# Order of the matmuls with stationary weights: four of 512 columns, then four of 256, instead of pairs

## The chip, the cores and the metric

The kernel runs on one core of a Trainium2 chip. A core has five engines that take their own instruction lists and meet through semaphores: PE (TensorE, the matrix engine, with its weight loads shown apart as PEld), DVE (VectorE), ACT (ScalarE), POOL (GpSimd) and SP (SyncE, which issues most transfers here). The metric is the device time of one execution in microseconds.

## The reference

Two transformer blocks, one after the other, on 256 tokens of 2048 features, all in float32. Cut to the products:

```python
# first block: stick-breaking attention, then a squared-ReLU MLP
qkv = rms_norm(x) @ w_qkv                     # 2048 -> 6144
x = x + attention(qkv) @ w_o                  # 2048 -> 2048
x = x + square(relu(rms_norm(x) @ w1)) @ w2   # 2048 -> 8192 -> 2048
# second block: chunked attention and pooling, then a gated MLP with a causal convolution
z = rms_norm(x) @ w_in                        # 2048 -> 4096
x = x + rms_norm(concat(attention(z), pool(z)) @ w_o)
up = conv3(rms_norm(x) @ w_up)                # 2048 -> 11264
x = x + rms_norm((gelu(up[:5632]) * up[5632:]) @ w_down)
```

The two attention cores, the pooling and the norms are small beside these products.

## The kernel before

Float32 products are made from rounded parts. Every activation tile has a high part and a low part side by side, 256 tokens each, so 512 columns; every weight has a high part `Wh` and a low part `Wl`. A product is high times high, low times high and high times low.

The weights come in 745 **pieces**. A piece is 256 rows of a weight matrix by a strip of 512 output features (128 partitions by 1024 numbers, 512 KB). SP loads a piece into `raw` (6 buffers), ACT rounds it into `Wh` (line 811), DVE takes the rest into `Wl` (line 1023), and PE multiplies by both; there are 5 buffers of `Wh` and `Wl`. A plan written at build time fixes what every engine does in which order: up to four pieces are split ahead of the one that PE works on, and the evacuations, norms and attention steps are laid between the pieces. PE waits on the low part of a piece once, ahead of its first matmul, and the piece's last matmul releases its buffers (`p.mm`) and, in the last piece of a strip, the accumulated result.

There are three kinds of piece:

- **T pieces**, 576 of them, `feature_products`: the weights are stationary, the activations move. The piece has two slices of 128 weight rows (`t`), and each slice has four blocks of 128 output features (`m`), one to each of the four PSUM banks of the accumulator `P`. For each `m` there is a matmul with `Wh` over all 512 columns (high and low activations), and one with `Wl` over the 256 columns of the high activations, into the first half of the same bank. The four pairs of one slice are a row of four, so there are 1152 such rows.
- **N pieces**, `row_products`: the activations are stationary, the weights move. They consist of matmuls of 512 columns only.
- Two **P pieces**, `group_products`, for the pooling, with 8 pairs each.

In the trace a T pair is `ps<-aHL,Wh` (512 columns) and `ps<-aHL,Wl` (256 columns), or the same with `hid` or `oHL` as the moving tensor. All carry line 1332, which is the helper `mm`. Each matmul has its own weight load of 128 columns (LDWEIGHTS on PEld).

Of the kernel before, what the change touches and what calls it, by code (L numbers as in the profile page):

```python
# [11 lines left out]
TOK = 256  # L12
# [634 lines left out]
def build(nc, A, out):  # L647
    with ExitStack() as ctx:
# [84 lines left out]
        def attention_weights(g, blk, h, b, n):  # L733
            if blk == 1:
                return A1[:, g % 2, :, :].rearrange("p h n -> p (h n)").rearrange("p (b h q) -> p b h q", b=3, h=4)[:, b:b + n, h, :]
            return A2[:, g % 2, h, b * 128:(b + n) * 128]
# [593 lines left out]
        def tensor_program(e):  # L1330
            def mm(o, l, r, start, stop):
                return e.matmul(o, l, r, start=start, stop=stop, skip_group_check=True)  # L1332

            def tp(o, i):
                return e.transpose(o, i, ident[:, :])  # L1335

            def row_products(q, row, P):

                wh, wl, mov, kt = Wh[:, q["n"] % NW, :], Wl[:, q["n"] % NW, :], movs[q["mov"]], q["kt"]
                for t in range(2):  # L1340
                    c = slice(t * 512, (t + 1) * 512)
                    hi = mov[:, kt + t, row * 128:(row + 1) * 128]
                    lo = mov[:, kt + t, TOK + row * 128:TOK + (row + 1) * 128]
                    mm(P[:, row, :], hi, wh[:, c], q["first"] and t == 0, False)
                    mm(P[:, row, :], hi, wl[:, c], False, False)
                    m = mm(P[:, row, :], lo, wh[:, c], False, q["last"] and t == 1)
                return m

            def feature_products(q, P, half=None):

                wh, wl, mov, kt = Wh[:, q["n"] % NW, :], Wl[:, q["n"] % NW, :], movs[q["mov"]], q["kt"]
                for t in range(2):
                    if half:
                        e.wait_ge(*half[t])
                    x = mov[:, kt + t, :]
                    for m in range(4):
                        c = slice(t * 512 + m * 128, t * 512 + (m + 1) * 128)
                        mm(P[:, m, :], wh[:, c], x, q["first"] and t == 0, False)
                        r = mm(P[:, m, 0:TOK], wl[:, c], x[:, 0:TOK], False, q["last"] and t == 1)
                return r  # L1360

            def group_products(q, P):
# [10 lines left out]
            for st in p.steps:  # L1373
                k = st["kind"]
                if k == "products":
                    q = pieces[st["i"]]
                    P = ps[q["set"]]
# [4 lines left out]
                    if q["kind"] == "T":  # L1382
                        feature_products(q, P, (st["half"], st["lo"]) if st["half"] else None).then_inc(p.mm, 1)
                    elif q["kind"] == "P":
                        group_products(q, P).then_inc(p.mm, 1)
                    else:
                        for row in st["rows"]:
                            m = row_products(q, row, P)
                            if row == 0 and st["row0"]:
                                m.then_inc(p.row0, 1)  # L1390
                            if row == 1:
                                m.then_inc(p.mm, 1)
                elif k == "rms":
                    P = ps[st["set"]]
# [4 lines left out]
                    for t in range(2):  # L1399
                        m = mm(P[:, 0, t:t + 1], Z4[:, 0, t * 128:(t + 1) * 128], ones[:, 0:1], True, True)  # L1400
                    m.then_inc(st["total"][0], 1)
                elif k == "rms_pair":
                    P = ps[st["set"]]
# [5 lines left out]
                    for j in range(2):  # L1409
                        for t in range(2):  # L1410
                            m = mm(P[:, 0, 2 * j + t:2 * j + t + 1], Z4[:, j, t * 128:(t + 1) * 128], ones[:, 0:1], True, True)
# [12 lines left out]
                elif k == "sb_scores":  # L1424
                    g, P = st["g"], ps[st["set"]]
                    q, kk = qk[:, g % 2, 0, :, :], qk[:, g % 2, 1, :, :]
                    for t in st["need"]:
                        e.wait_ge(*t)
                    for h in range(4):
                        for b, (i, j) in enumerate(BLOCKS):  # L1430
                            m = mm(P[:, b, h * 128:(h + 1) * 128], kk[:, h, i * 128:(i + 1) * 128],
                                   q[:, h, j * 128:(j + 1) * 128], True, True)
                    m.then_inc(st["mm"][0], 1)
                elif k == "sb_weights":
                    g, P = st["g"], ps[st["set"]]
                    for t in st["need"]:
                        e.wait_ge(*t)
                    for b, terms in enumerate((((tri_r, 0),), ((tri_r, 1), (ones_r, 2)), ((tri_r, 2),))):
                        for n, (l, at) in enumerate(terms):
                            c = slice(at * 512, (at + 1) * 512)  # L1440
                            mm(P[:, b, :], l[:, :], E_hi[:, g % 2, c], n == 0, False)
                            m = mm(P[:, b, :], l[:, :], E_lo[:, c], False, n == len(terms) - 1)
                    m.then_inc(st["mm"][0], 1)
                elif k == "values":
                    g, blk, P = st["g"], st["blk"], ps[st["set"]]
# [3 lines left out]
                    for h in range(4):  # L1449
                        c = slice(h * 128, (h + 1) * 128)  # L1450
                        mm(P[:, h, 0:256], v[:, g % 2, 0, c], attention_weights(g, blk, h, 0, 2), True, False)
                        m = mm(P[:, h, 128:256], v[:, g % 2, 1, c], attention_weights(g, blk, h, 2, 1), False, True)
                    m.then_inc(st["mm"][0], 1)
                elif k == "sm_scores":
                    g, P = st["g"], ps[st["set"]]
                    q, kk = qk[:, g % 2, 0, :, :], qk[:, g % 2, 1, :, :]
                    for t in st["need"]:
                        e.wait_ge(*t)
                    for h in range(4):
                        mm(P[:, h, 0:128], q[:, h, 0:128], kk[:, h, 0:128], True, True)  # L1460
                        m = mm(P[:, h, 128:384], q[:, h, 128:256], kk[:, h, :], True, True)
                    m.then_inc(st["mm"][0], 1)
                elif k == "sm_turn":
                    for t in st["need"]:
                        e.wait_ge(*t)
                    for h in range(4):
                        for b in range(3):
                            m = tp(ps[st["set"]][:, h, b * 128:(b + 1) * 128], Z3[:, h, b * 128:(b + 1) * 128])
                    m.then_inc(st["mm"][0], 1)
                elif k == "mixed_norm":  # L1470
                    for n in range(14):
                        m = mm(ps[st["set"]][:, 3, 0:128], ones[:, :], ones[:, :], True, True)
                    m.then_inc(st["warm"][0], 1)
                elif k == "mixed_tiles":
                    j0, b0, P = st["j0"], st["b0"], ps[st["set"]]
                    for t in st["need"]:
                        e.wait_ge(*t)
                    for n, i in enumerate((0, 2)):
                        for a in range(2):
                            for t in range(2):  # L1480
                                j = j0 + i + a
                                m = mm(P[:, b0 + n, a * 256 + t * 128:a * 256 + (t + 1) * 128], xn[:, t, j * 128:(j + 1) * 128],
                                       D[:, t * 128:(t + 1) * 128], True, True)
                        m.then_inc(st["turns"][n][0], 1)
                elif k == "turn_x3":
                    c = st["c"]
# [3 lines left out]
                    for t in range(2):  # L1490
                        for j in range(8):
                            m = tp(ps[st["set"]][:, 2 * t + j // 4, (j % 4) * 128:(j % 4 + 1) * 128],
                                   xT[:, 8 * c + j, t * 128:(t + 1) * 128])
# [56 lines left out]
```

## Time and profile before

| | |
|---|---|
| median of 3 runs | 2157.34 us |
| lowest and highest | 2157.23 and 2159.55 us |
| the profiled execution, its own time | 2159.01 us |
| its span, first to last instruction | 2157.3 us |
| outside the span | 1.7 us |
| mean granted TensorE clock | 0.997 |
| PE busy | 2132.7 us, 99%, 11698 matmuls |
| PE weight loads busy | 1850.3 us, 86% |
| DVE busy | 1285.3 us, 60% |
| ACT busy | 1065.0 us, 49% |

A matmul's record begins where it is started and reaches past the start of the next one, since matmuls are pipelined. So a duration of 0.39 us is not what a matmul costs; what it costs is the distance from its start to that of the next. Where the records of one form follow each other, a count over a stretch, or the first and last start, gives that distance.

### The profile page before, as it was taken

The numbers are of one execution on the slowest core, as the hardware profiler recorded it, in microseconds if no ns is written. First come the engines' busy times: TensorE is split into PE (matmuls) and PEld (weight loads), VectorE is DVE, ScalarE is ACT, GpSimd is POOL, SyncE is SP. The second block draws the span as 40 slices with busy tenths as digits, with TensorE's granted clock in tenths as the row PEclk, the third lists the DMA queues.
The fourth block names the chain that finished last, engine by engine and source line by source line (L and its number), as shares of the span: only waits on it lengthen the run. The fifth ranks groups of instructions, "written<-read, shape, count | busy, mean of one in ns | idle before, by whom it ended". The sixth has DMA issues, their size and how long they took to land.

```text
span 2157.3 us, 28152 instructions
## 1 busy us (share of the span) xinstructions
PE 2132.7 (99%) x11698; PEld 1850.3 (86%) x11698; DVE 1285.3 (60%) x1335; ACT 1065.0 (49%) x1198; POOL 240.5 (11%) x135
## 2 busy tenths in 40 slices
PE   8999999999999999999999999999999999999998
PEld 7888888888888888888888888888888888888886
DVE  6555556655555565555669655576666644566654
ACT  6554554545334443444554545455455433554553
POOL 2000000100000000000224000032222100222211
PEclk9999999999999999999999999999999999999999
DMA  8456555565666655665565655645655666566563
GB/s 274 152 167 190 170 174 185 167 207 174 207 190 183 197 185 190 176 207 193 187 198 172 183 169 177 193 137 186 189 191 180 213 194 193 168 186 200 193 199 111
DMA packets 207472, 399.50 MB, mean 185 GB/s; under 512 B 12400, under 2 KB 15600, under 8 KB 207088
## 3 DMA queue, kind: packets, MB, share of 16 engines
q1 hardware_dynamic: 207056, 395.60, 57.9%
q8 instruction: 92, 1.51, 0.3%
q10 hardware_dynamic: 288, 2.10, 0.2%
q14 instruction: 36, 0.29, 0.0%
HBM read 395.55 MB, written 2.10 MB: 184 GB/s over the span
## 4 chain that ended last, share of the span: by engine, by line
PE 95%; POOL 1%; issue 1%; DVE 1%; ACT 1%; DMA 0%; SPq 0%; DVEq 0%; POOLq 0%; ACTq 0%
PE ps L1332 94%; POOL T L1301 0%; PE ps L1335 0%; DMA raw<-in_sb_w_qkv_dram 0%; DVE raw L1230 0%; DVE Wl L1023 0%; POOL E L1257 0%; POOL T L1303 0%; POOL QK L1264 0%; POOL E L1292 0%; ACT Wh L811 0%; POOL zs L1267 0%; POOL QK L1257 0%; DVE T L978 0%; DVE xT L1101 0%
## 5 line engine op out<-in xcount | busy, mean ns | idle before, releaser
L1023 DVE TENSOR_TENSOR Wl<-raw,Wh 128x1024 fp32r<-128x1024 f32 x745 | 919.9, 1254 | 623.2 <-ACT Wh L811 622.4
L1332 PE MATMUL ps<-aHL,Wh 128*128 128x512 f32 x3328 | 1167.5, 395 | 11.5 <-DVE Wl L1019 6.6
L811 ACT ACTIVATE Wh<-raw 128x1024 fp32r<-128x1024 f32 x745 | 769.1, 1054 | 613.7 <-PE ps L1332 609.3
L1332 PE MATMUL ps<-aHL,Wl 128*128 128x256 f32 x3328 | 932.7, 280 | 0.0
L1332 PEld LDWEIGHTS ps<-aHL,Wh 128*128 128x128 f32 x3328 | 625.8, 188 | 155.6 <-DVE aHL L1013 6.5
L1332 PEld LDWEIGHTS ps<-aHL,Wl 128*128 128x128 f32 x3328 | 630.2, 189 | 0.4
L1332 PE MATMUL ps<-hid,Wh 128*128 128x512 f32 x1024 | 355.1, 391 | 0.0
L1332 PE MATMUL ps<-hid,Wl 128*128 128x256 f32 x1024 | 286.7, 280 | 0.0
L1332 PEld LDWEIGHTS ps<-hid,Wh 128*128 128x128 f32 x1024 | 191.5, 187 | 42.0
L1332 PE MATMUL ps<-Wh,hid 128*128 128x512 f32 x704 | 217.6, 389 | 0.0
L1332 PEld LDWEIGHTS ps<-hid,Wl 128*128 128x128 f32 x1024 | 193.5, 189 | 0.0
L1332 PEld LDWEIGHTS ps<-Wh,hid 128*128 128x128 f32 x704 | 132.1, 188 | 27.3
L1332 PE MATMUL ps<-Wl,hid 128*128 128x512 f32 x352 | 137.0, 389 | 0.0
L1332 PE MATMUL ps<-Wh,aHL 128*128 128x512 f32 x384 | 121.4, 392 | 0.5 <-DVE Wl L1023 0.5
L1257 POOL TENSOR_TENSOR E<-E 128x512 f32<-128x512 f32 x8 | 11.6, 1452 | 954.3 <-ACT E L815 954.3
L1310 POOL TENSOR_TENSOR T<-T,r_b 128x1024 f32<-128x1024 f32 x22 | 71.0, 3229 | 400.2 <-DVE T L978 392.4
L978 DVE TENSOR_TENSOR T<-ps,T 128x1024 f32<-128x1024 f32 x54 | 66.0, 1223 | 55.8 <-ACT T L785 54.3
L1332 PE MATMUL ps<-oHL,Wh 128*128 128x512 f32 x272 | 94.6, 394 | 0.0
L785 ACT ACTIVATE T<-ps 128x1024 f32<-128x1024 f32 x54 | 55.2, 1022 | 67.2 <-PE ps L1332 66.6
L1332 PEld LDWEIGHTS ps<-Wh,aHL 128*128 128x128 f32 x384 | 72.1, 188 | 15.9 <-DVE Wl L1023 0.9
L1332 PE MATMUL ps<-Wh,oHL 128*128 128x512 f32 x256 | 79.5, 390 | 0.0
L1332 PEld LDWEIGHTS ps<-Wl,hid 128*128 128x128 f32 x352 | 66.1, 188 | 13.7
(170 smaller groups left out, 1287.3 us busy)
## 6 DMA issues: line engine op xcount, KB each, us to landing
raw<-in_mlp_w_dram SPq DMA_DIRECT2D x256, 512.0 KB, 4.2
raw<-in_w_up_dram SPq DMA_DIRECT2D x176, 512.0 KB, 3.9
raw<-in_sb_w_qkv_dram SPq DMA_DIRECT2D x95, 512.0 KB, 4.6
raw<-in_w_down_dram SPq DMA_DIRECT2D x88, 512.0 KB, 4.1
raw<-in_w_in_dram SPq DMA_DIRECT2D x64, 512.0 KB, 4.1
raw<-in_sb_w_o_dram SPq DMA_DIRECT2D x32, 512.0 KB, 4.4
raw<-in_w_o_dram SPq DMA_DIRECT2D x32, 512.0 KB, 4.0
xT<-in_x_dram SPq DMA_DIRECT2D x8, 256.0 KB, 7.5
```

The costliest lines, as they stand in the source:

```text
L785: e.activation(T0[:, :, :], ps[st["set"]][:, :, TOK:2 * TOK], ACT.Copy).then_inc(st["copied"][0], 1)
L811: e.activation(Wh[:, i % NW, :], rawv[:, i % NRAW, :], ACT.Copy).then_inc(st["hi"][0], 1)
L978: e.tensor_tensor(T1[:, :, :], ps[st["set"]][:, :, 0:TOK], T0[:, :, :], ALU.add).then_inc(st["summed"][0], 1)
L1023: e.tensor_tensor(Wl[:, i % NW, :], rawv[:, i % NRAW, :], Wh[:, i % NW, :].bitcast(F32), ALU.subtract).then_inc(st["lo"][0], 1)
L1257: e.tensor_tensor(B[:, 0:2, :], B[:, 0:2, :], B[:, 2:4, :], ALU.add).then_inc(st["half"][0], 1)
L1310: e.tensor_tensor(T1[:, :, :], T1[:, :, :], rows4("r_b"), ALU.mult).then_inc(st["done"][0], 1)
L1332: return e.matmul(o, l, r, start=start, stop=stop, skip_group_check=True)
```

## The change

In `feature_products` the loop over the four blocks `m` is cut in two. Before, each turn issued the 512-column matmul with `Wh` and then the 256-column matmul with `Wl` of the same block. Now the four matmuls with `Wh` come first, one to each bank, and then the four with `Wl`.

```diff
                     x = mov[:, kt + t, :]
+                    cs = [slice(t * 512 + m * 128, t * 512 + (m + 1) * 128) for m in range(4)]
                     for m in range(4):
-                        c = slice(t * 512 + m * 128, t * 512 + (m + 1) * 128)
-                        mm(P[:, m, :], wh[:, c], x, q["first"] and t == 0, False)
-                        r = mm(P[:, m, 0:TOK], wl[:, c], x[:, 0:TOK], False, q["last"] and t == 1)
+                        mm(P[:, m, :], wh[:, cs[m]], x, q["first"] and t == 0, False)
+                    for m in range(4):
+                        r = mm(P[:, m, 0:TOK], wl[:, cs[m]], x[:, 0:TOK], False, q["last"] and t == 1)
                 return r
```

On PE, at the start of the program, where the first piece has a wait ahead of each slice, the list before reads:

```order
1 L1332 MATMUL ps<-aHL,Wh 128x512 [waits s_half_lo,s_tile_lo]
2 L1332 MATMUL ps<-aHL,Wl 128x256
3 L1332 MATMUL ps<-aHL,Wh 128x512
4 L1332 MATMUL ps<-aHL,Wl 128x256
5 L1332 MATMUL ps<-aHL,Wh 128x512
6 L1332 MATMUL ps<-aHL,Wl 128x256
7 L1332 MATMUL ps<-aHL,Wh 128x512
8 L1332 MATMUL ps<-aHL,Wl 128x256
9 L1332 MATMUL ps<-aHL,Wh 128x512 [waits s_w_lo]
10 L1332 MATMUL ps<-aHL,Wl 128x256
```

and after the change, at the same place:

```order
1 L1332 MATMUL ps<-aHL,Wh 128x512 [waits s_half_lo,s_tile_lo]
2 L1332 MATMUL ps<-aHL,Wh 128x512 x3
3 L1332 MATMUL ps<-aHL,Wl 128x256 x4
4 L1332 MATMUL ps<-aHL,Wh 128x512 [waits s_w_lo]
5 L1332 MATMUL ps<-aHL,Wh 128x512 x3
6 L1332 MATMUL ps<-aHL,Wl 128x256 x4
7 L1332 MATMUL ps<-aHL,Wh 128x512 [waits s_w_lo,s_tile_lo]
```

The waits stand before the same matmul as before, the first of a slice; only the seven behind it have changed places.

On PE, where the strips of the gated MLP's first half end and the N pieces of the down projection (`ps<-Wh,hid`) begin, before:

```order
8735 L1332 MATMUL ps<-aHL,Wh 128x512
8736 L1332 MATMUL ps<-aHL,Wl 128x256
8737 L1332 MATMUL ps<-aHL,Wh 128x512
8738 L1332 MATMUL ps<-aHL,Wl 128x256
8739 L1332 MATMUL ps<-Wh,hid 128x512
8740 L1332 MATMUL ps<-Wl,hid 128x512
```

and after:

```order
2784 L1332 MATMUL ps<-aHL,Wl 128x256 x4
2785 L1332 MATMUL ps<-aHL,Wh 128x512 x4
2786 L1332 MATMUL ps<-aHL,Wl 128x256 x4
2787 L1332 MATMUL ps<-Wh,hid 128x512
2788 L1332 MATMUL ps<-Wl,hid 128x512
```

The last matmul of the strip is the same one as before, with `Wl` of block 3, and the N pieces behind it have not moved. The numbers of matmuls of each form are the same in both kernels, and ACT, DVE, POOL and SP have the same lists.

## Rows read from the trace of the kernel before

**Rows 1.** The page: PE and weight loads, and the chain by engine.

```profile
PE 2132.7 (99%) x11698; PEld 1850.3 (86%) x11698; DVE 1285.3 (60%) x1335; ACT 1065.0 (49%) x1198; POOL 240.5 (11%) x135
PE 95%; POOL 1%; issue 1%; DVE 1%; ACT 1%; DMA 0%; SPq 0%; DVEq 0%; POOLq 0%; ACTq 0%
```

**Rows 2.** Groups, PE: line, form, count | busy us, mean ns | idle before.

```profile
L1332 PE MATMUL ps<-aHL,Wh 128*128 128x512 f32 x3328 | 1167.5, 395 | 11.5 <-DVE Wl L1019 6.6 <-DVE T L978 3.2 <-DVE aHL L1185 1.3
L1332 PE MATMUL ps<-aHL,Wl 128*128 128x256 f32 x3328 | 932.7, 280 | 0.0
```

**Rows 3.** Timeline, PE, T pieces, from 600 us: start us, us, what.

```profile
599.91 0.39 PE L1332 MATMUL ps<-hid,Wh 128*128 128x512 f32 x1
600.14 0.28 PE L1332 MATMUL ps<-hid,Wl 128*128 128x256 f32 x1
600.25 0.39 PE L1332 MATMUL ps<-hid,Wh 128*128 128x512 f32 x1
...
602.68 0.39 PE L1332 MATMUL ps<-hid,Wh 128*128 128x512 f32 x1
```

**Rows 4.** Timeline, PEld, weight loads of the same stretch.

```profile
600.14 0.19 PEld L1332 LDWEIGHTS ps<-hid,Wh 128*128 128x128 f32 x1
600.26 0.19 PEld L1332 LDWEIGHTS ps<-hid,Wl 128*128 128x128 f32 x1
```

**Rows 5.** Timeline, PE, N pieces, matmuls of 512 columns alone.

```profile
2100.37 0.39 PE L1332 MATMUL ps<-Wl,hid 128*128 128x512 f32 x1
2100.59 0.61 PE L1332 MATMUL ps<-Wh,hid 128*128 128x512 f32 x2
2101.05 0.39 PE L1332 MATMUL ps<-Wl,hid 128*128 128x512 f32 x1
...
2102.41 0.39 PE L1332 MATMUL ps<-Wl,hid 128*128 128x512 f32 x1
```

**Rows 6.** Timeline, PE, T pieces at the lower clock.

```profile
1184.34 0.63 PE L1332 MATMUL ps<-aHL,Wh 128*128 128x512 f32 x1
1184.77 0.41 PE L1332 MATMUL ps<-aHL,Wl 128*128 128x256 f32 x1
1184.98 0.63 PE L1332 MATMUL ps<-aHL,Wh 128*128 128x512 f32 x1
```

**Rows 7.** Timeline, PE, first five and last four of 24 matmuls of the scores.

```profile
63.67 0.72 PE L1332 MATMUL ps<-QK 128*128 128x128 f32 x5
...
65.89 0.61 PE L1332 MATMUL ps<-QK 128*128 128x128 f32 x4
```

**Rows 8.** Stretches: us, then PE, PEld, DVE, ACT, POOL busy (count), PEclk, DMA, GB/s.

```profile
14.00:44.00 30.00, 30.00 (x172) 26.00 (x171) 21.70 (x23) 22.08 (x27) 9.11 (x7) 1.00 0.88 306
450.00:600.00 150.00, 150.00 (x867) 132.25 (x866) 85.53 (x72) 68.93 (x67) 0.00 (x0) 1.00 0.60 196
1500.00:1650.00 150.00, 150.00 (x867) 132.29 (x866) 95.05 (x120) 78.78 (x94) 38.45 (x11) 1.00 0.60 190
1850.00:2000.00 150.00, 150.00 (x851) 130.13 (x850) 91.62 (x113) 78.55 (x94) 36.47 (x10) 1.00 0.59 186
1808.00:2034.00 226.00, 226.00 (x1281) 196.06 (x1280) 138.38 (x168) 114.81 (x134) 47.51 (x13) 1.00 0.59 183
```

**Rows 9.** Stretch at the lower clock, the columns of rows 8.

```profile
1184.50:1186.50 2.00, 2.00 (x8) 1.71 (x7) 2.00 (x3) 0.00 (x0) 0.00 (x0) 0.50 0.49 171
```

**Rows 10.** Timeline, PE, T pieces in the stretch with fewer matmuls.

```profile
1899.70 0.40 PE L1332 MATMUL ps<-aHL,Wh 128*128 128x512 f32 x1
...
1900.76 0.40 PE L1332 MATMUL ps<-aHL,Wh 128*128 128x512 f32 x1
...
1901.82 0.40 PE L1332 MATMUL ps<-aHL,Wh 128*128 128x512 f32 x1
```

## Prediction, made before the run

> **What bounds the kernel now.** I read the page first. PE is busy 99% of the span and holds 95% of the chain that ended last [rows 1]. The groups then say where PE ever stood idle: 11.5 us before the first form of T matmul, nothing before the second [rows 2]. So no semaphore, transfer or other engine is worth asking about. The time is the sum of the distances between matmul starts, and the change can only act through those. The durations in the groups (395 and 280 ns) overlap and are of no use for this; the timeline's starts are.
>
> In T pieces at 600 us the starts of the 512-column matmuls go from 599.91 to 602.68 over 8 pairs: 346 ns a pair, split 0.23 + 0.11 or 0.12 [rows 3]. The count over 150 us says the same: 867 matmuls are 173 ns each, 346 ns a pair [rows 8]. Over 150 us the rounding is small, and a few overlapping records at the edges make the count about two too high; with 865 it is 346.8. I use 346.7. In N pieces, 512 columns only, 9 matmuls take 2102.41 - 2100.37 = 2.04 us, 226.7 ns each [rows 5]. If a 512-column matmul costs the same in a T pair, the 256-column one costs 346.7 - 226.7 = 120 ns.
>
> What part of this is streaming? At a granted clock of 0.50 (the 1.2 GHz level) a pair takes 1184.98 - 1184.34 = 0.64 us [rows 6, 9], so 0.32 us at the 2.4 GHz level if nothing is added. Measured there is 346.7: 26.7 ns above it, for two matmuls. For the N matmul the same ratio gives 320 x 512/768 = 213.3, and 226.7 is 13.4 above it. So every matmul, long or short, carries about 13.3 ns besides its columns, at the full clock alone. A fixed charge for each matmul with its weight load fits all three rows.
>
> Each load starts with the matmul ahead of it (600.14 and 600.26, against matmuls at 600.14 and 600.25) and is 190 ns long on record, yet the 512-column matmul starts 0.11 us after the load for it [rows 3, 4]. So the record's length is not what a load holds up. The pace of loads shows in the attention scores, where 24 matmuls of 128 columns follow each other, each with its load: from the first at 63.67 to the 21st at 65.89 are 20 distances, 111 ns each [rows 7]. I take 112 as the most that a load can hold up. It lies below 120.
>
> **The change part by part.** *Matmuls and loads*: none is added or removed. A row of four is 4 x 226.7 + 4 x 120 = 1386.8 ns before. After, it has the same eight in another order. With a charge per matmul the sum is the same to the nanosecond: difference 0, times 1152 rows, 0 us.
>
> *Cover of the loads.* A load runs beside the matmul ahead of it. Before, four loads lay under 512-column matmuls and four under 256-column ones. After, it is still four and four, since the cover is given by the matmul ahead, and the same eight are ahead of something. The four under short ones have 120 ns of cover for 112 ns of need. What is new is that three of them follow each other. A load starts only once the matmul ahead starts, so a surplus under a long matmul was never carried over and none is lost: 0 us. In the scores, 24 loads went in a row at their pace [rows 7], so issuing instructions keeps up with four short matmuls too.
>
> *PSUM.* Before, both matmuls of a pair went to the same bank; after, each goes to another bank than the one ahead. N pieces write one bank six times in a row at 226.7 ns, with the same 13.3 ns charge as T pairs that change bank every second time [rows 3, 5]. So a bank has no price here either way: 0 us.
>
> *Waits and releases.* The waits stand ahead of the first matmul of a slice as before, and the last matmul of a piece is the same instruction, so the buffers of `Wh` and `Wl` and the strip's result come free when they did. DVE is busy 60%, ACT 49% [rows 1]; nothing in their work moves. 0 us.
>
> *The rhythm.* One thing in the trace isn't explained by a fixed charge. From 1808 to 2034 us the T pieces run slower with the same instructions: 851 matmuls in 150 us where 867 ran before [rows 8]. Three pairs take 1900.76 - 1899.70 = 1.06 us, 353.3 ns a pair [rows 10]. It isn't the company of other engines: 1500 to 1650 us holds the same stage's work (POOL 38.45 against 36.47 us, ACT 78.78 against 78.55) and runs at 867 [rows 8]. So a stream of pairs can settle into either of two rhythms, 6.7 ns a pair apart. What a new order settles into isn't in this trace. Bounds: if all slow stretches went, the one of rows 8 gives 226/353.3 x 6.7 = 4.3 us and the one from 14 to 44 us (172 matmuls, where the usual pace has 173 and the two at the edges, 175) 0.6 us. A few others are shorter; I put them at 50 us together, 0.9 us, so 5.8 us in all. If all T pairs took the slow rhythm, 4608 pairs less some 870 already slow (306 us / 353.3) make 3740 x 6.7 = 25.1 us more. I take 0 between them: the steady form is by far the more common.
>
> *Sum*: 0 us on the span of 2157.3 us of the profiled execution, whose own time was 2159.01. The median of the runs is 2157.34, and the forecast is made on that: 2157.3 us. The runs of before differ by 2.3 us, so a change under 0.2% (4.3 us) can't be told from none.
>
> **The rivals.**
>
> *Short matmuls in a row run at the load pace (faster).* The 120 ns is a difference between two forms; no row shows a 256-column matmul behind another. If a run of them needs only its load pace, 3 of the 4 fall from 120 to 112: 24 ns a row, x 1152 = 27.6 us, 2129.7 us. If they only fall to the 0.117 seen between starts [rows 3], it is 3 x 3.3 x 1152 = 11.4 us, 2145.9 us. For it: the distances 0.23 and 0.117 leave it open how the charge is shared. Against: 226.7 in N pieces fixes the long one at 13.3 ns, and the rest must then be in the short one.
>
> The Trainium skill, TensorE: Matmul & The Clock Gate, Back-to-back issue gap, lists 262 cycles for 256 columns, which is 109 ns at 2.4 GHz, and its section LDWEIGHTS (loading the stationary operand) has a load of 128 columns take 128/1.2 = 107 ns. An estimate from that page puts four short matmuls in a row at 109 ns each and would gain some 38 us over three in each row. Its gap doesn't agree with this trace for 512 columns, where it has 518 cycles, 216 ns, and the rows show 226.7, so I follow the rows and leave this rival a small chance.
>
> *The slow stretches vanish (slightly faster).* They began behind N pieces; a row that changes between long and short twice instead of eight times may fall out of the slow rhythm. 2157.3 - 5.8 = 2151.5 us.
>
> *The new order settles into a slower rhythm (slower).* The mechanism: each switch from a run of short matmuls to a run of long ones upsets the phase between the loads and the moving stream, and the long ones need several to settle, as the stream of pairs in rows 10 never does. It decides if a row costs over 3.7 ns more than 1386.8 (4.3 us / 1152). At the slow rhythm throughout it is 2157.3 + 25.1 = 2182.4 us; half of it is 2169.9.
>
> *Loads become the bound in full (much slower).* If the fourth of four needed its whole 190 ns on record, three a row would cost 70 ns more: 210 x 1152 = 242 us, 2399 us. Rows 3 and 4 show a 512-column matmul starting well inside its load's record, so this has next to no chance.
>
> **How the numbers follow.** Chances: unchanged sum 0.43 (2153 to 2161.6), load pace or part of it 0.18 (2130 to 2150), slow stretches gone 0.13 (2151.5, its edge in the band of no change), slower rhythm 0.25 (2161.6 to 2182), loads in full 0.01. Faster by over 0.2% is 0.18 + 0.13 less 0.01 at the edge = 0.30; within, 0.44; slower 0.26. The range: 2136 leaves out about a third of the first rival (0.06), 2175 a third of the slower one and the last (0.09). The unchanged sum has its own range of 2153 to 2161.6, given since the two signs beside it hold over half.
>
> **What would show it.** In the changed kernel's timeline: long matmuls at 226.7 ns in a run of four and short ones at 120, a row from first to first at 1387, and 865 to 867 T matmuls in 150 us. A short run at 112 to 117 shows the first rival; over 120, or long ones at 230 to 240 behind a short run, the slower one. Loads that start later than the matmul ahead, or idle time on PE over 11.5 us, would upset the whole reading. The last stretch, 1808 to 2034, tells whether the slow rhythm is still there.

## The result and the profile after

The change makes the kernel slower: 2171.43 us median of 4 runs (2171.06 to 2171.77) against 2157.35 (2157.23 to 2159.55). The ratio is 1.0062, with a 95% interval of 1.005 to 1.0074. The profiled execution took 2171.70 us, with a span of 2170.0, so the span grew by 12.7 us.

The page of the changed kernel, to be held against [rows 1]: busy time, and the chain by engine.

```profile
PE 2145.8 (99%) x11698; PEld 1856.4 (86%) x11698; DVE 1285.5 (59%) x1335; ACT 1065.0 (49%) x1198; POOL 240.5 (11%) x135
PE 95%; POOL 1%; issue 1%; DVE 1%; ACT 1%; DMA 0%; SPq 0%; DVEq 0%; POOLq 0%; ACTq 0%
```

The group of long matmuls after, with the idle time before it (line, form, count | busy us, mean ns | idle us). Its busy time isn't to be held against [rows 2]: long matmuls now overlap each other, and where records overlap the time is counted once.

```profile
L1332 PE MATMUL ps<-aHL,Wh 128*128 128x512 f32 x3328 | 913.8, 396 | 10.9 <-DVE Wl L1019 6.4
```

The number of instructions is the same, PE's busy time grew by 13.1 us, and the idle time is 10.9 us where it was 11.5 [rows 2]. No wait was added. The matmuls themselves stand further apart, as these three stretches of the changed kernel show (us; then PE, PEld, DVE, ACT, POOL busy with counts, PEclk, DMA, GB/s):

```profile
450.00:600.00 150.00, 150.00 (x857) 131.11 (x856) 83.86 (x70) 70.04 (x69) 0.00 (x0) 1.00 0.59 190
850.00:1000.00 150.00, 150.00 (x857) 131.09 (x856) 83.58 (x70) 67.58 (x66) 0.00 (x0) 1.00 0.60 185
1850.00:2000.00 150.00, 150.00 (x857) 131.10 (x856) 94.34 (x119) 79.79 (x96) 34.35 (x10) 1.00 0.59 183
```

Before, 150 us held 867 matmuls in most of the program and 851 in its slow stretch [rows 8]. Now they hold 857 everywhere, at the same granted clock of 1.00. Timeline of the changed kernel, PE (start us, us, what; equal instructions in a row are merged):

```profile
599.42 1.09 PE L1332 MATMUL ps<-hid,Wh 128*128 128x512 f32 x4
600.35 0.63 PE L1332 MATMUL ps<-hid,Wl 128*128 128x256 f32 x4
600.82 1.09 PE L1332 MATMUL ps<-hid,Wh 128*128 128x512 f32 x4
601.75 0.64 PE L1332 MATMUL ps<-hid,Wl 128*128 128x256 f32 x4
602.23 1.09 PE L1332 MATMUL ps<-hid,Wh 128*128 128x512 f32 x4
```

Two rows of four take 602.23 - 599.42 = 2.81 us. From the starts in the trace's records, in ns, they are

```
long 233 236 228 233   short 117 119 118 116   row 1400
long 235 234 236 224   short 117 120 120 120   row 1406
```

and rows of these two kinds take turns, 1403.3 ns on average over the 150 us from 450 us, 16.5 more than the 1386.8 of the prediction. Over the same stretch the distance from a long one's start to the next start is 232.3 ns on average, that from a short one's 118.5. How this splits depends on what one holds it against. Against 226.7 and 120, the figures of the prediction, the long ones lose 22 ns a row and the short ones give back 6. Against the kernel before, where the same records give 230.0 behind a long one's start and 116.7 behind a short one's (0.23 and 0.11 or 0.12 in [rows 3]), the long ones lose 9 ns a row and the short ones 7. Only the sum of a row can be compared without choosing. Over 1152 rows the 16.5 ns are 19.0 us. The slow stretches of before, worth 5.8 us, are gone. 19.0 - 5.8 = 13.2 us, and the span grew by 12.7.

### The profile page after: what moved, and what is told of

It is laid out like the page before. It is cut to its first block, busy times and chain, and to the rows that moved or that the text cites. A ratio compares the mean times of both kernels' runs of the same rounds, so it can differ in the third digit from the quotient of the medians.

```text
span 2170.0 us, 28152 instructions
## 1 busy us (share of the span) xinstructions
PE 2145.8 (99%) x11698; PEld 1856.4 (86%) x11698; DVE 1285.5 (59%) x1335; ACT 1065.0 (49%) x1198; POOL 240.5 (11%) x135
## 4 chain that ended last, share of the span: by engine, by line
PE 95%; POOL 1%; issue 1%; DVE 1%; ACT 1%; DMA 0%; SPq 0%; DVEq 0%; POOLq 0%; ACTq 0%
PE ps L1332 94%; POOL T L1301 0%; DMA raw<-in_sb_w_qkv_dram 0%; PE ps L1335 0%; DVE raw L1230 0%; DVE Wl L1023 0%; POOL E L1257 0%; POOL T L1303 0%; POOL QK L1264 0%; POOL E L1292 0%; ACT Wh L811 0%; POOL zs L1267 0%; POOL QK L1257 0%; DVE T L978 0%; DVE xT L1101 0%
## 5 line engine op out<-in xcount | busy, mean ns | idle before, releaser
L1332 PE MATMUL ps<-aHL,Wh 128*128 128x512 f32 x3328 | 913.8, 396 | 10.9 <-DVE Wl L1019 6.4
L1332 PEld LDWEIGHTS ps<-aHL,Wh 128*128 128x128 f32 x3328 | 571.7, 189 | 88.8 <-DVE aHL L1013 6.4
L1332 PEld LDWEIGHTS ps<-aHL,Wl 128*128 128x128 f32 x3328 | 512.4, 189 | 71.4
L1332 PE MATMUL ps<-aHL,Wl 128*128 128x256 f32 x3328 | 530.7, 281 | 0.0
L1332 PE MATMUL ps<-hid,Wh 128*128 128x512 f32 x1024 | 279.5, 394 | 0.0
L1332 PEld LDWEIGHTS ps<-hid,Wh 128*128 128x128 f32 x1024 | 175.0, 189 | 23.5
L1332 PEld LDWEIGHTS ps<-hid,Wl 128*128 128x128 f32 x1024 | 157.1, 189 | 21.8
L1332 PE MATMUL ps<-hid,Wl 128*128 128x256 f32 x1024 | 162.9, 281 | 0.0
L1332 PE MATMUL ps<-oHL,Wh 128*128 128x512 f32 x272 | 75.6, 395 | 0.0
```

## Experiments

Each edit is shown against `feature_products` of the kernel before, where the body of a slice is the loop over `m`. `H` stands for the matmul with `Wh` over 512 columns and `L` for the one with `Wl` over 256.

### Runs of two and runs of eight

```diff
-for m in range(4): H(t, m); L(t, m)
+for a in (0, 2): H(t, a); H(t, a+1); L(t, a); L(t, a+1)
```

> The row of four is ordered 2 x 512, 2 x 256, 2 x 512, 2 x 256 columns. Theory A (a fixed cost of some 16.7 ns each time the stream comes back from short matmuls to long ones in runs): a piece has 4 returns instead of 2, so 2840 ns instead of 2807, in all about 2190 us. Theory B (each short matmul that stands behind a short one costs some 2.8 ns, because its load has only 120 ns of cover; 12 such in a piece after the change, 4 here): 2784 ns a piece, 2158 us. Theory C (a change of PSUM bank costs some 4 ns; each matmul changes bank here as in the changed kernel): 2807 ns, 2171 us.

Measured: 2159.85 us median of 8, ratio 1.0004 (0.9993 to 1.0015). A piece takes 2786.7 ns in the steady state. Theory A was far off (2840). B had 2784 and 2158 us. Theory C, a price for each change of bank, had 2807 and falls too, as every matmul changes bank here.

```diff
-for t in range(2):
-    for m in range(4): H(t, m); L(t, m)
+for t in range(2):
+    for m in range(4): H(t, m)
+for t in range(2):
+    for m in range(4): L(t, m)
```

> Both slices of a piece are joined: 8 matmuls of 512 columns, then 8 of 256. Theory A (cost per return from short to long): one return a piece, 2790 ns, about 2161 us. Theory B (cost per short behind short): 14 in a piece instead of 12, 2812 ns, 2174 us. Theory C (bank changes): as the changed kernel, 2807 ns, 2171 us.

Measured: 2163.48 us median of 8, ratio 1.0024 (1.0013 to 1.0035). A piece takes 2793.3 ns, near A's 2790, while B's 2812 and C's 2807 fail. So neither A nor B fits both orders. Timeline of the kernel with eights, PE:

```profile
599.83 1.30 PE L1332 MATMUL ps<-hid,Wh 128*128 128x512 f32 x5
600.97 1.11 PE L1332 MATMUL ps<-hid,Wl 128*128 128x256 f32 x8
601.92 2.00 PE L1332 MATMUL ps<-hid,Wh 128*128 128x512 f32 x8
603.76 1.12 PE L1332 MATMUL ps<-hid,Wl 128*128 128x256 f32 x8
```

Eight long ones take 603.76 - 601.92 = 1.84 us, while the last five of the eight before them took 600.97 - 599.83 = 1.14, 228 each. So the first three of a run take some 0.70, 233 each. The trace's starts give the run in full:

```
long  233 236 229 232 231 227 226 227   short 113 119 120 120 120 120 120 120   ns
```

In this order, behind a run of short matmuls, the first five long ones are 2 to 9 ns too slow, 28 ns in all, and only the sixth is back at the N pieces' 227. The switch from long to short gives 7 ns back. A row of four never gets to a settled part. This is not a fixed price for each switch, though: runs of two switch twice as often as runs of four and cost less.

### Short matmuls alone

```diff
-for m in range(4): H(t, m); L(t, m)
+for m in range(4): H256(t, m); L(t, m)     # H over the 256 high columns only, but whole in a strip's first slice
```

> Leaves the low activations times the high weights out in all slices but a strip's first, so that nearly all matmuls with stationary weights have 256 columns and the pitch of short matmuls in an unbroken run can be read. Theory A: 120 ns, as worked out from the pairs. Theory B: more than 120 ns, since loads fall behind. If the load pace is what counts: 112 ns. At 120 ns the pieces take 1920 ns, and the whole some 1660 us, if the transfers keep up; the pitch within a piece is what counts.

Timeline of the kernel with short matmuls alone:

```profile
491.20 0.28 PE L1332 MATMUL ps<-hid,Wl 128*128 128x256 f32 x1
491.32 0.28 PE L1332 MATMUL ps<-hid,Wh 128*128 128x256 f32 x1
...
493.12 0.28 PE L1332 MATMUL ps<-hid,Wl 128*128 128x256 f32 x1
```

16 distances in 493.12 - 491.20 = 1.92 us: 120 ns each, as in theory A and as the prediction had worked out. A run doesn't go at the load pace of 112. The whole took 1853 us, since PE now waits for weights between pieces, which the expectation had allowed for. Theory B in its plain form is out: short matmuls behind short ones cost nothing by themselves.

### One bank or four

```diff
-L(t, m)
+L(t, (m + 2) % 4)      # in a strip's first slice: H, H, H, H, L, L, L, L
```

> The alternating order of before, 512 then 256 columns, but the 256-column matmul goes to the bank two further on, so every matmul changes bank as in the changed kernel. (The first slice of a strip has the changed kernel's order.) Theory C (bank changes cost): as slow as the changed kernel, some 1403 ns a row, 2171 us. Theories A and B: the pair stays at 346.7 ns or at the slow 353.3, 2151 to 2165 us.

Measured: 2168.68 us median of 4, ratio 1.0045 (1.0025 to 1.0065). That looked like theory C, but the trace says otherwise. Timeline of this kernel, PE, from two neighbouring strips of the same weights:

```profile
719.95 0.40 PE L1332 MATMUL ps<-aHL,Wh 128*128 128x512 f32 x1
...
724.19 0.40 PE L1332 MATMUL ps<-aHL,Wh 128*128 128x512 f32 x1
```

```profile
737.60 0.39 PE L1332 MATMUL ps<-aHL,Wh 128*128 128x512 f32 x1
...
741.76 0.39 PE L1332 MATMUL ps<-aHL,Wh 128*128 128x512 f32 x1
```

The rows between are the other pairs, 12 distances in each: 4.24 us, 353.3 ns a pair, in the one strip, and 4.16 us, 346.7, in the next. All matmuls change bank in both. Through most of the program the strips take turns between the two rhythms, and what stands at each border is the strip's first slice, the one with its four long matmuls first. The same eight matmuls send a fast stream into the slow rhythm and a slow one into the fast. So the grouped slice was the suspect, not the bank. The edit that does the bank alone leaves that slice out:

```diff
-L(t, m)
+L(t, (m + 2) % 4)      # in a strip's first slice: L(t, m), alternating as before
```

> The alternating order of before in every slice, with the short matmul two banks further on except in a strip's first slice. If only the phase of the stream counts, the order 512, 256 keeps its rhythm whatever the bank: 346.7 ns a pair where before had it, 2157 us. If a change of bank cost some 4 ns, 4 more changes a row: 2171 us.

Measured: 2157.93 us median of 8, ratio 1.0000 (0.9988 to 1.0011). Its stretches have the counts of the kernel before [rows 8], the fast ones and the slow one:

```profile
450.00:600.00 150.00, 150.00 (x868) 132.25 (x866) 85.22 (x72) 68.12 (x67) 0.00 (x0) 1.00 0.60 196
1850.00:2000.00 150.00, 150.00 (x851) 129.98 (x851) 92.12 (x114) 79.01 (x95) 36.47 (x10) 1.00 0.59 185
```

So no price of a change of bank shows.

### One grouped slice in the whole program

```diff
+if (q["n"], t) == (160, 0): H, H, H, H, L, L, L, L
+else: H, L, H, L, H, L, H, L
```

> The order of before, except for a single slice, in piece 160 at about 490 us, in the middle of 800 us at 346.7 ns a pair. Theory P: that one slice of eight matmuls throws all pairs behind it into the slow rhythm, up to the next wait of PE at about 1125 us: 1830 pairs x 6.7 = 12 us, some 2169 us. Rival S: the slice costs its own 17 ns at most, no change in time.

Measured: 2168.91 us in one run, beside 2158.69 (median of 13) for the kernel before. Timeline around the slice, PE:

```profile
485.42 0.39 PE L1332 MATMUL ps<-aHL,Wh 128*128 128x512 f32 x1
485.65 0.28 PE L1332 MATMUL ps<-aHL,Wl 128*128 128x256 f32 x1
485.77 1.09 PE L1332 MATMUL ps<-aHL,Wh 128*128 128x512 f32 x4
486.69 0.64 PE L1332 MATMUL ps<-aHL,Wl 128*128 128x256 f32 x4
487.17 0.40 PE L1332 MATMUL ps<-aHL,Wh 128*128 128x512 f32 x1
...
488.23 0.40 PE L1332 MATMUL ps<-aHL,Wh 128*128 128x512 f32 x1
```

and a later stretch of it, where before held 867 or 868:

```profile
850.00:1000.00 150.00, 150.00 (x851) 130.12 (x850) 83.05 (x70) 67.32 (x65) 0.00 (x0) 1.00 0.59 185
```

The slice takes 487.17 - 485.77 = 1.40 us, 13 ns over a usual row. The three pairs behind it take 488.23 - 487.17 = 1.06 us, the slow rhythm. By the trace's starts the slow rhythm is a cycle of three pairs: 233, 117, 241, 120, 236, 113 ns. It holds for some 1830 pairs, to 1135.9 us, where eight matmuls of one column (`ps<-ones,zs`) come between the pairs; behind them the pairs are at 346.7 again. Eight matmuls in another order cost 10 us in this one run, several hundred times what they cost on the spot. Theory P gave 2169. Rival S falls.

```diff
+if (q["n"], t) in ((2, 0), (627, 0)): H, H, H, H, L, L, L, L
+else: H, L, H, L, H, L, H, L
```

> The order of before, except that one slice in piece 2 and one in piece 627 (behind the N pieces, where the slow rhythm of 353.3 ns a pair began) have their four long matmuls first. Theory P (the stream of pairs has a phase that holds by itself, 346.7 or 353.3 ns a pair, and one grouped slice shifts it): behind each of the two slices pairs run at 346.7 ns, the slow stretch of 226 us goes, 4 to 5 us less than before, about 2153 us. Rival S (the slow rhythm belongs to that stage's other work or data): it stays, no change.

Measured: 2153.60 us median of 10 (2152.95 to 2155.25), ratio 0.9977 (0.9968 to 0.9987). Timeline around the slice in piece 627, and the stretch of [rows 8] that had 851:

```profile
1808.35 0.40 PE L1332 MATMUL ps<-aHL,Wh 128*128 128x512 f32 x1
...
1809.41 0.40 PE L1332 MATMUL ps<-aHL,Wh 128*128 128x512 f32 x1
...
1810.11 1.11 PE L1332 MATMUL ps<-aHL,Wh 128*128 128x512 f32 x4
1811.05 0.63 PE L1332 MATMUL ps<-aHL,Wl 128*128 128x256 f32 x4
1811.52 0.40 PE L1332 MATMUL ps<-aHL,Wh 128*128 128x512 f32 x1
...
1812.57 0.39 PE L1332 MATMUL ps<-aHL,Wh 128*128 128x512 f32 x1
```

```profile
1850.00:2000.00 150.00, 150.00 (x868) 131.11 (x866) 94.71 (x119) 79.11 (x95) 37.13 (x11) 1.00 0.60 189
```

Ahead of the slice three pairs take 1.06 us, behind it 1.05 and then 346.7 a pair, and the stretch is at 868 matmuls with the same work beside it. The other slice, in piece 2, did not lift the slow rhythm there, against theory P's expectation for it, so a slice is a push and not a cure. That it counts where in the rhythm the slice falls is my reading, not shown by itself. This kernel is 0.23% faster than the one before and 0.8% faster than the changed one, by the two medians.

The two traces also show a rhythm that changes with no slice near. Between the stream that holds to 1123 us and the stretch below, both kernels have the same instructions in the same order: pairs, the one-column matmuls, and one wait of PE of 0.90 or 0.91 us. Both come in at 346.7 ns a pair. The kernel before leaves at 346.7, the other at 353.3. First the kernel before, then the one with two slices:

```profile
1135.00:1175.00 40.00, 40.00 (x233) 34.98 (x232) 39.34 (x42) 16.60 (x18) 22.56 (x12) 1.00 0.60 182
```

```profile
1135.00:1175.00 40.00, 40.00 (x228) 34.66 (x227) 38.43 (x41) 16.47 (x17) 22.94 (x12) 1.00 0.60 182
```

### Halved loads

```diff
-L: mm(P[:, m, 0:256], wl[:, 128 columns], ...)
+L: mm(P[0:64, m, 0:256], wl[:, first 64 of them], ...)
```

with the order of before:

> The order of before, but the matmuls of 256 columns load only 64 of their 128 weight columns and write only half the output rows, so half of the low weights' part is left out. Theory L (the 13.3 ns beside the columns are taken by the load from the moving stream, in step with its size): 6.7 ns less a pair, 340 ns, 31 us less, about 2126 us. Rival F (a fixed cost for each matmul): 346.7 ns a pair, 2157 us.

Measured: 2155.52 us in one run. Nearly everywhere a pair takes 346.7 ns, as the fixed cost F has it, in the stretch that was slow before too (868 matmuls from 1850 to 2000 us). But from 1131 to 1176 us, behind the same wait of PE, it took 340, theory L's figure:

```profile
1140.13 0.39 PE L1332 MATMUL ps<-aHL,Wh 128*128 128x512 f32 x1
1140.36 0.27 PE L1332 MATMUL ps<-aHL,Wl 128*64 128x256 f32 x1
...
1142.17 0.39 PE L1332 MATMUL ps<-aHL,Wh 128*128 128x512 f32 x1
```

Six pairs in 2.04 us. So even the charge of 13.3 ns that I took as fixed isn't: with smaller loads there is a third rhythm, 6.7 ns lower still. Which of F and L is right stays open; the stream can run either way.

With the changed kernel's order and the same halved loads:

> The changed kernel's order with the same halved loads for the matmuls of 256 columns (half of the low weights' part left out). If the extra 16.7 ns a row come from loads that fall behind under the short matmuls, they vanish here: 1387 ns a row with rival F or 1360 with theory L. If they come from long matmuls that settle behind any run of short ones, they stay: 1403 ns a row (F) or 1377 (L).

Measured: 2152.40 us in one run. Timeline, PE:

```profile
599.86 1.08 PE L1332 MATMUL ps<-hid,Wh 128*128 128x512 f32 x4
600.79 0.62 PE L1332 MATMUL ps<-hid,Wl 128*64 128x256 f32 x4
601.25 1.08 PE L1332 MATMUL ps<-hid,Wh 128*128 128x512 f32 x4
602.17 0.63 PE L1332 MATMUL ps<-hid,Wl 128*64 128x256 f32 x4
602.63 0.86 PE L1332 MATMUL ps<-hid,Wh 128*128 128x512 f32 x3
```

Two rows take 602.63 - 599.86 = 2.77 us, 1386.7 a row by the records: the extra 16.5 ns are gone, in the stretches from 450, 850 and 1850 us alike. Then the loads of the long matmuls were halved instead:

> The changed kernel's order, with the loads of the 512-column matmuls halved instead (64 of 128 weight columns, except in a strip's first slice; half of the high weights' part is left out), those of the short ones whole. If what costs 16.7 ns a row is the whole load of a short matmul laid under a short one, it stays: 1403 ns a row, about 2170 us. If the size of any load near the switch decides, 1387 ns a row, about 2153 us.

Measured: 2166.50 us in one run, with 858 matmuls in 150 us where the changed kernel has 857:

```profile
450.00:600.00 150.00, 150.00 (x858) 115.74 (x857) 84.16 (x71) 68.71 (x68) 0.00 (x0) 1.00 0.59 193
```

A row takes 1399 ns by the records, so 12.5 of the extra 16.5 ns stay. What makes the changed order dearer than pairs hangs on the short matmuls having their whole loads; the loads of the long ones have a small part in it. Two things stay open here. A halved load comes with a matmul that writes half the output rows, and no run parts the two. And all four short loads of a row were halved, so it isn't shown that the three under short matmuls are the ones that count; the next run speaks against it.

### Four long ones and a single short one

```diff
-for m in range(4): H(t, m); L(t, m)
+for m in range(4): H(t, m)
+L(t, 3)
```

> Each row has its four 512-column matmuls and only one of 256 (three of the four low-weight products are left out). By the charge per matmul a row is 4 x 226.7 + 120 = 1026.8 ns. If long matmuls need to settle behind any short one, as the eights showed it (28 ns over the first five long ones, 7 given back at the switch), some 1045 ns. If it takes a run of short ones to upset them, 1027 ns. The total, near 1740 us if the transfers keep up, tells less than the row.

Timeline, PE:

```profile
600.53 0.28 PE L1332 MATMUL ps<-aHL,Wl 128*128 128x256 f32 x1
600.64 1.08 PE L1332 MATMUL ps<-aHL,Wh 128*128 128x512 f32 x4
601.57 0.28 PE L1332 MATMUL ps<-aHL,Wl 128*128 128x256 f32 x1
```

This row takes 1.04 us. Where the stream is undisturbed a row takes some 1037 or some 1047 ns, 1041.5 on average, 15 more than the charge per matmul gives. The total, 1889.94 us, says little, since PE waits for weights there. So a run of short ones isn't needed, nor a short matmul's load under another short one: here the only short load lies under a long matmul. Nor is it the first long matmul that pays. In four rows on end the starts give

```
long 231 224 231 235   short 116
long 224 231 236 228   short 117
long 235 233 236 224   short 118
long 233 236 228 233   short 117   ns
```

and over the undisturbed rows from 560 to 1000 us the four places of a long matmul average 230.9, 231.2, 232.5 and 230.1. The loss is spread over the row.

All orders side by side, mean distance in ns from a start to the next, from 450 to 600 us at a granted clock of 1.00 where nothing else is said:

| order | behind a long start | behind a short start | four pairs |
|---|---|---|---|
| pairs | 230.0 | 116.7 | 1386.7 |
| pairs, slow rhythm, 1850 to 2000 us | 236.7 | 116.7 | 1413.3 |
| runs of two | 233.1 | 115.2 | 1393.3 |
| runs of four (the change) | 232.3 | 118.5 | 1403.3 |
| runs of eight | 230.1 | 119.1 | 1396.7 |
| pairs, short loads halved | 229.2 | 117.5 | 1386.7 |
| the same, 1131 to 1176 us | 227.0 | 113.0 | 1360.0 |
| runs of four, short loads halved | 230.7 | 115.9 | 1386.7 |
| runs of four, long loads halved | 229.8 | 120.1 | 1399.5 |

Halving the short loads in runs of four took 1.6 ns off each long distance and 2.6 off each short one.

## Why the prediction was wrong

- **The bound** was right: no wait and no other engine came into it, PE's busy time grew with the span, and the distances between starts carried all of the change.
- **Cost of a short matmul**: right for a run of them: 120 ns were forecast, and 120 is what an unbroken run takes. The first rival (112 or 117 ns in a run) fell with it. But in pairs the distance behind a short start is 116.7 and behind a long one 230.0, as [rows 3] already had it (0.23, and 0.11 or 0.12). So 226.7 + 120 gave the right sum of a pair from parts that a pair doesn't have.
- **The fixed charge per matmul**: this is the step that failed. The prediction gave each matmul 13.3 ns besides its columns in any order, and wrote the difference down as 0 "to the nanosecond". The same eight matmuls took 1386.7 ns in pairs, 1393.3 in twos, 1396.7 in eights and 1403.3 in fours. What a matmul costs depends on those around it. Two effects that break such a charge were looked at beside it, and both were put at 0: the next two.
- **Cover of the loads**: put at 0, since four loads lie under long and four under short ones in any order. Halving just the short matmuls' loads took the extra cost away (1386.7 a row), halving the long ones' left most of it (1399). So the loads aren't free in this order. Which of the short loads count isn't shown.
- **The rhythm**: put at 0, measured at 16.5 ns a row, 19.0 us, less the 5.8 us of the slow stretches. I had seen the two rhythms and bounded the term at 25 us upward, then took 0 because the steady form was the more common *in the old order*. That says nothing on a new one. No row showed a run of long matmuls behind a run of short ones, so the likeliest value had no support.
- **PSUM banks**: right, by the bank alone at a ratio of 1.0000 and by the same counts in the stretches.
- **Waits and releases, issue**: right, by the idle time and the same 857 in all stretches.
- **The rivals**: the slower one, at a chance of 0.25, is the one that came true. Its mechanism is right in part: the stream is upset behind short matmuls, and in the eights the long ones take five to settle. But the cost is no price of a switch, as the twos show, and in a row with a single short one it is spread. Its half-way value of 2169.9 us is near the measured 2171.4 by luck: it was half the way to the slow rhythm of pairs, 13.3 ns a row, and the changed order runs in a rhythm of its own. The second, that the slow stretches vanish, came true beside it (857 in all stretches) and took back some 5.8 us. The rival of loads as the full bound (2399 us) was rightly given next to no chance.
- **The range**, 2136 to 2175, held the time only because it reached into the slower rival.

What is shown: the order alone makes the difference, no bank and no wait has a part in it, the difference to pairs is gone where the short matmuls have half their loads, and a stream of pairs keeps a rhythm until something shifts it. The rhythm can also change where other matmuls and a wait of PE come between the pairs, as the stretch from 1135 to 1175 us shows (233 and 228 matmuls for the same instructions). What is not shown: what inside the engine has this phase, why fours cost more than twos and eights, and which of the short loads count. The kernel before spread from 2156.6 to 2163.2 us on one chip, 6.6 us, which is what slow stretches of other lengths would make, but only one of its executions was traced, so this stays argued.

## What to carry to other kernels

Where PE is never idle, the order of its matmuls is a term of its own, and its price can't be read from the same instructions in another order. A long and a short moving operand in turn took 346.7 ns here, as much as one of each from unbroken runs (226.7 + 120), while runs of two, eight and four cost 6.7, 10 and 16.5 ns more for each four pairs. Count matmuls over equal stretches of the same form: where the counts differ at the same clock, a rhythm has slipped, and a few matmuls in another order at its start can push it back (2153.6 us, 0.23% less, for one slice that did so). The same push in the wrong place cost 10 us.

## What the runs showed of the hardware

- A stream of alternating matmuls of 512 and 256 columns has at least two rhythms that hold by themselves with the same instructions, 346.7 and 353.3 ns a pair, and a third of 340 where the short ones' loads were halved. One slice of eight matmuls in another order switched it for 1830 pairs.
- A run of matmuls of 256 columns takes 120 ns each, one of 512 columns 226.7. That is 13.3 ns over the columns in both, at the upper of the clock's two levels alone [rows 6, 9], and it isn't fixed: with the short ones' loads halved a pair also ran at 340, so at 227 + 113.
- In runs of eight, long matmuls behind short ones take 233, 236, 229, 232 and 231 ns before they are back at 227.
- The Trainium skill, TensorE: Matmul & The Clock Gate, Back-to-back issue gap, lists 518 cycles for 512 columns and 262 for 256, which is 216 and 109 ns at 2.4 GHz; it calls them the gap of isolated matmuls, without a budget for their loads. This kernel's rounded float32 operands, each with its load, ran at 226.7 and 120 in unbroken runs, so the measurement decides, and the estimate of 109 ns in the prediction doesn't hold.
